# First attention scores placed between the value projection's last products, and the attention output's norm and transposes begun head by head in the last tiles

## The reference, cut to what matters

```python
# one layer; 512 latent tokens and 128 prompt tokens share the projections
proj = h @ w_in                                    # q_r k_r v_r g_r q_d k_d v_d gates
q_d = apply_rope(q_d, cos_d, sin_d); k_d = apply_rope(k_d, cos_d, sin_d)   # latent tokens only
# differential attention, 8 heads, two maps m of 64 columns each
s = einsum('bqhmd,bkhmd->bhmqk', q, k) * dh ** -0.5
p = softmax(s); a = p[:, :, 0] - lam * p[:, :, 1]
o = einsum('bhqk,bkhe->bqhe', a, v)
o_d = rmsnorm(o, diff_subln_g) * (1 - lam_init)    # per head, 128 columns
branch_d = o_d.reshape(B, L, 1024) @ w_diff_out
mix = (gate_r * branch_r + gate_d * branch_d) @ w_o
# then residual, RMSNorm, SwiGLU FFN, residual, final norm
```

## Time and profile before

| what | us |
|---|---|
| median of 3 runs (1314.15 to 1314.39) | 1314.18 |
| the profiled execution, its own time | 1314.83 |
| its span in the trace | 1313.2 |
| PE busy | 1263.9 (96%) |
| DVE busy | 798.2 (61%) |
| ACT busy | 487.5 (37%) |
| POOL busy | 307.6 (23%) |

### The profile page before, as it was taken

The page is one execution under the profiler, slowest core; times in us unless marked ns, Lnnn a source line. Parts: engine busy times, 40 slices in busy tenths (PEclk is TensorE's granted clock), DMA queues, the critical chain, the costliest instruction groups (busy, mean ns, idle before and its releaser), DMA issues.

```text
span 1313.2 us, 19818 instructions
## 1 busy us (share of the span) xinstructions
PE 1263.9 (96%) x7734; PEld 1155.6 (88%) x7734; DVE 798.2 (61%) x1292; ACT 487.5 (37%) x812; POOL 307.6 (23%) x269
## 2 busy tenths in 40 slices
PE   4999999999999999999799899999999999999997
PEld 2698887799999999988688799889998999989986
DVE  4654121466657733463799754378984689547966
ACT  5452223344331112222777532245441244313434
POOL 1011000311000111120699700003520355005500
PEclk9999999999999999999899999999999999999999
DMA  9634222144444434362000034220233122322222
GB/s 307 206 97 136 64 74 71 41 148 141 127 131 130 142 104 127 106 192 97 33 1 1 10 121 153 88 64 27 71 119 106 33 81 89 120 64 64 89 89 80
DMA packets 87392, 129.56 MB, mean 99 GB/s; under 512 B 3529, under 2 KB 64450, under 8 KB 87186
## 3 DMA queue, kind: packets, MB, share of 16 engines
q1 hardware_dynamic: 76880, 95.17, 22.7%
q0 software_dynamic: 9104, 32.20, 8.0%
q10 hardware_dynamic: 1330, 1.10, 0.3%
HBM read 117.43 MB, written 4.73 MB: 93 GB/s over the span
## 4 chain that ended last, share of the span: by engine, by line
PE 85%; POOL 6%; DVE 4%; ACT 3%; issue 1%; DMA 1%; SPq 0%; ACTq 0%; DVEq 0%
PE psum L421 31%; PE psum L458 28%; PE psum L664 17%; POOL probs L961 4%; POOL probs L967 3%; PE psum L1024 1%; PE psum L407 1%; DMA ada_a<-in_w_ada 1%; PE psum L594 1%; PE psum L522 1%; DVE w_lo L390 1%; PE psum L1132 1%; PE psum L1130 1%; PE psum L1131 0%; ACT probs L1531 0%
## 5 line engine op out<-in xcount | busy, mean ns | idle before, releaser
L390 DVE TENSOR_TENSOR w_lo<-w_raw,w_hi 128x2048 fp32r<-128x2048 f32 x57 | 130.6, 2291 | 200.9 <-ACT w_hi L385 197.6
L385 ACT ACTIVATE w_hi<-w_raw 128x2048 fp32r<-128x2048 f32 x57 | 108.8, 1909 | 173.7 <-PE psum L458 107.5
L421 PE MATMUL psum<-h_hi,w_lo 128*128 128x320 f32 x672 | 154.7, 311 | 0.8 <-ACT y_nat L1474 0.8
L421 PE MATMUL psum<-h_hi,w_hi 128*128 128x320 f32 x672 | 153.1, 309 | 0.0
L421 PE MATMUL psum<-h_lo,w_hi 128*128 128x320 f32 x672 | 153.0, 309 | 0.0
L458 PE MATMUL psum<-w_hi,hid 128*128 128x512 f32 x440 | 135.5, 389 | 0.0
L421 PEld LDWEIGHTS psum<-h_hi,w_lo 128*128 128x128 f32 x672 | 111.8, 188 | 1.7 <-issue 1.7
L421 PEld LDWEIGHTS psum<-h_lo,w_hi 128*128 128x128 f32 x672 | 112.3, 188 | 0.0
L421 PEld LDWEIGHTS psum<-h_hi,w_hi 128*128 128x128 f32 x672 | 112.3, 188 | 0.0
L664 PE MATMUL psum<-h_hi,seven_lo 128*128 128x320 f32 x320 | 98.9, 309 | 1.1 <-DVE silu_g L2189 1.1
L664 PE MATMUL psum<-h_lo,seven_hi 128*128 128x320 f32 x320 | 98.9, 309 | 0.0
(11 more groups left out here) (302 smaller groups left out, 2771.7 us busy)
## 6 DMA issues: line engine op xcount, KB each, us to landing
w_raw<-in_w_in SPq DMA_DIRECT2D x32, 1024.0 KB, 5.5
ada_b<-in_w_ada POOLq DMA_DIRECT2D x32, 512.0 KB, 4.0
w_raw<-in_w_ffn_gate SPq DMA_DIRECT2D x11, 1024.0 KB, 5.4
w_raw<-in_w_ffn_up SPq DMA_DIRECT2D x11, 1024.0 KB, 5.4
ada_a<-in_w_ada SPq DMA_DIRECT2D x8, 1024.0 KB, 13.3
w_raw<-in_w_ffn_down SPq DMA_DIRECT2D x8, 1024.0 KB, 5.1
w_raw<-in_w_ret_out SPq DMA_DIRECT2D x4, 1024.0 KB, 5.2
swapped<-qk_d POOLq DMA_DIRECT2D x32, 128.0 KB, 2.6
```

The costliest lines, as they stand in the source:

```text
L385: act.activation(w_hi[s][:, :, :], w_raw[s][:, :, :], ACT.Copy).then_inc(w_hi_done, 1)
L390: dve.tensor_tensor(w_lo[s][:, :, :], w_raw[s][:, :, :], w_hi[s][:, :, :].bitcast(F32), ALU.subtract).then_inc(w_lo_done, 1)
L421: last = pe.matmul(bank(4 * par + 2 * j + h, HALF), w[:, k, cs], x[:, k, h * HALF:(h + 1) * HALF], start=(k == 0 and n == 0), stop=(k == K ...
```

## The change

The change does the following, on each engine:

- **PE.** The waits for `rope_done` and for the cached keys come ahead of v_d. In v_d's last group both modulation sums stand at the end of the first half, followed by the scores of tile 0. In the second half the token tiles go in the order 0, 2, 1, 3, 4, with a transpose of the gate columns after tile 0, the scores of tile 1 after tile 1, and the scores of tile 2 after tile 3. The loop then begins at slot 2. The transposes of the prompt's keys go to slot QT+1, the first block of the output's transposes to slot QT+2.
- **ACT.** It copies v_d's last five tiles between the exponentials of tiles 0 to 2. The high part of diff_out's first unit is made in 4 parts in slots 8 to 11. The roots for heads 0 to 6 come in slot QT, the copy of the prompt's keys in slot QT+1, the root of head 7 after the first block.
- **DVE.** The late modulation begins once its four sums are copied. The low part of diff_out's first unit is made in 8 parts in slots 14 to 21. The means and inverses of heads 0 to 6 come in slots QT and QT+1, heads 0 to 3 are scaled in slots QT+1 and QT+2, heads 4 to 7 between the low parts. Its wait for the stored prompt keys goes from the prompt groups to diff_out.
- **POOL** issues the gate vector's DMA ahead of the attention and the prompt keys' DMA after it, and scales no heads. **SP** issues the prompt values' DMA, and loads diff_out's first weights once the transposes of tiles 0 to 2 are done, because the weights of tiles 0 to 2 (`first_probs`) lie over the two raw weight buffers.

```diff
+LAST_TILES = (0, 2, 1, 3, 4)
+EARLY_HEADS = 7
+ACT_SPLIT_SLOTS, DVE_SPLIT_SLOTS = range(8, 12), range(14, 22)
-        k_out = at("k_out", H + 16, [P, D])
+        k_out = at("k_out", H + 25, [P, D])
+        first_probs = at("first_probs", W, [P, 3, 2, TOK])
+        def weights_of(n, m):
+            return (first_probs if n < 3 else probs)[:, n % 3, m, :]
+        def dve_split_part(dve, unit, s, part, parts):
+            ks = slice(part * KT // parts, (part + 1) * KT // parts)
+            if part == 0:
+                dve.wait_ge(w_hi_done, unit + 1)
+            done = dve.tensor_tensor(w_lo[s][:, ks, :], w_raw[s][:, ks, :], w_hi[s][:, ks, :].bitcast(F32), ALU.subtract)
+            if part == parts - 1:
+                done.then_inc(w_lo_done, 1)
...
 # pe_wide
-                        for t in range(TILES):
+                        for t in LAST_TILES if between and (i, par) == (1, 1) else range(TILES):
+                            if between and (i, par) == (1, 1):
+                                between(t)
+                    if between and i == 1:
+                        if par == 0:
+                            pe.wait_ge(freed[r], START[name][r] + TILES)
+                            pe.wait_ge(ada_step, 16 * (ADA_FIRST[name] + 3) + 32)
+                            for slot in range(2):
+                                last = sums_over_partitions(pe, slot, bank(1, 4, 4 * slot))
+                            last.then_inc(mm_done, 2)
+                            between(None)
+                        else:
+                            last.then_inc(mm_done, 2)
+                        continue
...
 # PE
             pe_dense(pe, "k_d", pe_T_unit, h_hi, h_lo)
-            pe_wide(pe, "v_d", h_hi, h_lo)
-            pe.wait_ge(freed["act"], START["diff_out"]["act"])
             pe.wait_ge(rope_done, 12 + AHEAD)
-            for h in range(DH):
-                last = pe.transpose(bank(6 + h // 4, P, (h % 4) * P), qk_d[:, DH + h, LAT:TOK], ident[:, :])
-            last.then_inc(k_ps, 1)
-            pe.wait_ge(ld_vc, 16)
             pe.wait_ge(kc_done, 1)
 # scores(n)
+                if n == 1:
+                    pe.wait_ge(freed["act"], START["v_d"]["act"] + TILES + 3)
+                if n == 2:
+                    pe.wait_ge(ada_copied, 4)
 # PE loop
-            pe.wait_ge(k_copied, 1)
-            for slot in range(-1, QT + 4):
+            def early_scores(t):
+                if t == 0:
+                    pe.wait_ge(gate_cols_set, 2)
+                    pe.wait_ge(at_max, 1)
+                    pe.transpose(psum[0:4 * KT, BANK:BANK + P], gate_cols[:, :, :, :].rearrange("p g c m -> p (g c m)"),
+                                 ident[:, :]).then_inc(gate_T_ps, 1)
+                if t == 3:
+                    pe.wait_ge(gate_T_set, 1)
+                if t in (None, 1, 3):
+                    scores((None, 1, 3).index(t))
+            pe_wide(pe, "v_d", h_hi, h_lo, between=early_scores)
+            for slot in range(2, QT + 4):
                 if 0 <= slot - 3 < QT:
                     weights_T(slot - 3)
+                if slot == QT + 1:
+                    prompt_keys_T()
                 if 0 <= slot - 4:
                     outputs(slot - 4)
+                if slot == QT + 2:
+                    pe.wait_ge(k_copied, 1)
+                    pe.wait_ge(at_e, 2 * QT)
+                    pe.wait_ge(norm["normo"]["scaled"], 1)
+                    tiles_T(pe, "od", o_nat, 0, 2)
                 if slot + 1 < QT:
                     scores(slot + 1)
             pe.wait_ge(at_oe, QT)
+            pe_T_and_dense(pe, "od", o_nat, "diff_out", od_hi, od_lo, by_block=norm["normo"]["scaled"], begun=1)
...
 # ACT
+            act_split(act, unit_of("v_d", 1, 1), 1)
+            act.wait_ge(mm_done, 2 * unit_of("v_d", 1, 0) + 2 + AHEAD)
+            for par in range(2):
+                copy_ada("v_d", 1, par, bank(1, 4, 4 * par)).then_inc(ada_copied, 1)
             set_table(ACT.Exp)
+            act.wait_ge(w_lo_done, unit_of("v_d", 1, 1) + 1)
+            exp(0)
...
+            v_d_tiles(1, (0, 2, 1))
+            exp(1)
+            v_d_tiles(1, (3,))
+            exp(2)
+            v_d_tiles(1, (4,))
+            for slot in range(3, QT + 3):
+                evacuate_T(slot - 3)
                 if slot < QT:
                     exp(slot)
+                if slot in ACT_SPLIT_SLOTS:
+                    act_split_part(act, unit_of("diff_out", 0, 0), 0, slot - ACT_SPLIT_SLOTS.start, len(ACT_SPLIT_SLOTS))
                 if slot == QT:
                     set_table(ACT.Sqrt)
+                    root("normo", EARLY_HEADS * TILES)
+                if slot == QT + 1:
+                    keys_out()
...
 # DVE, behind factor, evacuate_o and maximum of the slot
+                if slot in DVE_SPLIT_SLOTS:
+                    dve_split_part(dve, unit_of("diff_out", 0, 0), 0, slot - DVE_SPLIT_SLOTS.start, len(DVE_SPLIT_SLOTS))
+                if slot == QT:
+                    head_means(0, EARLY_HEADS)
+                if slot == QT + 1:
+                    head_inverses(0, EARLY_HEADS, 1)
+                if QT < slot < QT + 3:
+                    for h in (2 * (slot - QT - 1), 2 * (slot - QT) - 1):
+                        scale_head(dve, h).then_inc(norm["normo"]["scaled"], 1)
+            head_means(EARLY_HEADS, DH)
+            for k in range(KT):
+                split_T(dve, "od", od_hi, od_lo, subln_gain, k)
+                if k + 4 == EARLY_HEADS:
+                    head_inverses(EARLY_HEADS, DH, 2)
+                if k + 4 < DH:
+                    scale_head(dve, k + 4).then_inc(norm["normo"]["scaled"], 1)
```

More of the change, by code:

```diff
@@ L71 @@
 WIDE_BANKS = ((0, 1, 2, 6, 7), (3, 4, 5, 6, 7))
+LAST_TILES = (0, 2, 1, 3, 4)
+EARLY_HEADS = 7
 def wide_ready(name, i, t):
-    return (2 * WIDE.index(name) + i) * LAT_TILES + t + 1
+    place = LAST_TILES.index(t) if (name, i) == ("v_d", 1) else t
+    return (2 * WIDE.index(name) + i) * LAT_TILES + place + 1
 def lay_out_phases():
@@ L438, in wide, with pe_wide @@
             return w[:, 2 * k:2 * k + 2, :].rearrange("p a b -> p (a b)")
-        def pe_wide(pe, name, hi, lo, kt=KT, split=None):
+        def pe_wide(pe, name, hi, lo, kt=KT, split=None, between=None):
             r, half = READER[name][0], kt // 2
@@ L531, in block @@
                 if by_block is not None:
[L532 removed]
+                    pe.wait_ge(by_block, k + 1)
                 tiles_T(pe, which, src, k, 2 + 2 * (k % 3))
[L535 removed]
+            for k in range(begun, 3):
                 if which == "yg":
@@ L737, in norm2_low, with act_to_T @@
             dve.tensor_tensor(h2_lo[:, k, cs], hf2[:, k, cs], h2_hi[:, k, cs].bitcast(F32), ALU.subtract).then_inc(q["lo"], 1)
-        def act_to_T(act, which, hi, scale):
+        def act_to_T(act, which, hi, scale, blocks=range(KT)):
             q = n2t[which]
-            for k in range(KT):
+            for k in blocks:
                 act.wait_ge(q["ps"], k + 1)
@@ L841, in _ @@
             stream_wide("v_d", w_in, 5120)
+            sp.wait_ge(freed["act"], START["diff_out"]["act"])
+            sp.dma_start(o["new_diff_v"][0, 0].rearrange("p h e -> p (h e)"), v_d[:, LAT_TILES, :]).then_inc(vd_stored, 16)
+            sp.wait_ge(at_T, 3)
             stream("diff_out", columns(by_tile["w_diff_out"], 0))
@@ L1195, in weights_T @@
                     out = last_keys_T(n) if c == LAT_TILES else bank(6, P, c * P)
-                    last = pe.transpose(out, probs[:, n % 3, 0, c * P:(c + 1) * P], ident[:, :])
+                    last = pe.transpose(out, weights_of(n, 0)[:, c * P:(c + 1) * P], ident[:, :])
                 last.then_inc(at_T, 1)
             def outputs(n):
+                if n == 0:
+                    pe.wait_ge(freed["act"], START["diff_out"]["act"])
+                if n == GROUPS:
+                    pe.wait_ge(ld_vc, 16)
                 pe.wait_ge(at_aT, n + 1)
@@ L1434, in copy_N, with evacuate @@
             def copy_N(name, dst, func, after=0):
-                def evacuate(i):
+                def evacuate(i, tiles=range(TILES)):
                     if after:
                         act.wait_ge(rope_done, after + AHEAD)
-                    for t in range(TILES):
+                    for t in tiles:
                         wait_tile(act, name, i, t)
-                        if name in ADA_FIRST and t == LAT_TILES:
+                        if name in ADA_FIRST and t == LAT_TILES and i == 0:
                             copy_ada(name, i, 1, bank(ada_wide_bank(i, 1), 4)).then_inc(ada_copied, 1)
@@ L1513, in _ @@
             dense("k_d", copy_T("k_d", qk_d, DH, 1.0))
[L1514 to L1517, removed]
+            v_d_tiles = copy_N("v_d", v_d, ACT.Copy, after=12)
+            dense_wide("v_d", v_d_tiles, groups=1)
             def exp(n):
@@ L1849, in dense_wide @@
                             following()
```

(11 more changed lines are left out.)

89 lines of the change are left out of this document (43 added, 46 removed).

## The result

| kernel | median, us | range | runs |
|---|---|---|---|
| before | 1314.29 | 1313.43 to 1315.90 | 6 |
| after | 1319.83 | 1319.27 to 1320.71 | 6 |

The changed kernel is slower by 0.43%: the ratio is 1.0043, with a 95% interval of 1.0032 to 1.0054. The forecast was 1320.6, the difference +6.4 against a measured +5.5. The profiled execution took 1319.99 us, with a span of 1318.3; before, the span was 1313.2. So the trace has to account for 5.1 us. The times of the kernel before fall into two groups (of its 17 runs beside experiments 5 to 8, ten took 1313.3 to 1314.8 us at a mean granted clock of 0.995, seven 1315.3 to 1316.3 at 0.991 or 0.992), and the changed kernel is slower than both.

What follows compares the result with a forecast made beforehand. PE bounds the kernel almost throughout, POOL the attention, with slots nearly full on four engines. 9.2 + 2.5 - 9.0 + 6.9 + 0.2 - 3.4 = +6.4 on 1314.18 gives 1320.6 us; whole range 1313.5 to 1325.5.

Steps and rivals of the forecast that it cites:

- Steps 1 and 2: PE at v_d's front: waiting for the last key rotation costs 9.2 us, the lowered clock after that pause 2.5.
- Step 3: v_d's second half: scores placed between its tiles let POOL start its latent tiles earlier, -9.0 us (bounds -7 to -10.7).
- by tile 4: First latent tiles: next scores wait for one transposed tile only and PE avoids half clock, another 0.5 us gained.
- Step 4: Attention slots 14 to 21: DVE's eight low parts wait for POOL's add and delay its next tile, 0.87 each, +6.9 us.
- Rival A: Attention slots: the split parts don't meet POOL's add and cost 1.2 us, total 1314.9, no measurable change; chance 0.12.
- Step 5: Attention slots 8 to 11: ACT's four high parts, about 0.5 each against 0.53 of idle time, cost +0.2 us.
- Step 6: Tail after POOL's end: earlier transposes, DVE scaling heads between tiles and no POOL scaling save 3.4 us.
- Rival B: PE in front of v_d: the rotation wait is short, so the kernel gets faster, 1308.9 us; chance 0.05.
- Rival C: Attention: slots suffer beyond the parts, each of 12 losing another 0.3 to 0.5, about +5, 1325 us; chance 0.13.

Runs made afterwards that it cites:

- experiments 5 to 8: Late-wait kernel with scores behind v_d (1318.52), scaling behind last tile (1311.46), or low part in two pieces (1305.48); kernel before plus only the wait ahead of v_d (1325.58).
- experiment 2: Changed kernel with DVE's low part as one 128x2048 instruction in slot 14 instead of eight parts in slots 14 to 21: 1316.47 us.
- Experiment 3: Changed kernel with DVE's eight subtractions replaced by maximum reductions over the same 128x256 raw weights, leaving out that low part: 1315.35 us.
- experiment 7: Changed kernel with the rotation wait in front of tile 0's scores and DVE's low part in two 128x1024 pieces, slots 14 and 15: 1305.48 us.
- Experiment 6: Changed kernel with the late rotation wait, heads 0 to 3 scaled and block 0 transposed only after all tiles are evacuated: 1311.46 us.
- experiment 1: Changed kernel with PE's rotation wait moved from the front of v_d to the front of tile 0's scores: 1308.34 us.
- experiment 4: Changed kernel with both the rotation wait in front of tile 0's scores and DVE's low part in one piece: 1306.36 us.

## Why the prediction was right, by its steps

The steps as forecast and as the two traces and the runs have them:

| step | forecast | trace | by itself |
|---|---|---|---|
| 1. wait for the rotation | +9.2 | +8.8 | 1 and 2 together: 11.5 and 10.9 |
| 2. clock behind it | +2.5 | +2.2 | |
| 3. early scores | -9.0 | -7.8 | about 10 |
| 4. DVE's eight parts | +6.9 | +5.5 | 3.4 less in one piece |
| 5. ACT's four parts | +0.2 | +0.2 | not tried |
| 6. tail | -3.4 | -3.7 | 3.1 |
| sum | +6.4 | +5.2 | medians: +5.5 |

*Steps 1 and 2* held. v_d's first product moved by 572.28 - 563.45 = 8.83; The wait itself costs 0.4 more, about 9.3, because k_d's last product started 0.44 earlier than before (562.72 against 563.16). PE's pause of 9.10 is counted from that product's end. By the sums PE is 11.0 late, so the clock took 2.2. The forecast's 2.5 lay between two shorter half-speed stretches; here the pause was longest, yet only 4.4 us of work ran at half speed: the clock stood at 0.50 from 568.9 on, while PE was still idle. This size isn't fixed. Experiments 2 and 3 have the same code up to this place. There the half speed lasted 5.3 and 6.1 us, and PE came to the sums at 618.06 and 618.38, so the clock took 2.5 and 3.0.

*Step 3* was the right mechanism with its size 1.2 too large. The forecast let PE go from the sums to the end of v_d in 19.4 us (606.64 to 626.0); it took 637.97 - 617.64 = 20.3. The wait for tile 1's copy came out as forecast (0.69 idle), and the exponentials of tile 0 ended in v_d's cover. What was too small is each change of work on PE. The sums took 1.77 to the next start instead of 1.56. The first scores took 1.09 instead of 0.9, and the first product behind them 0.34 to its successor instead of 0.23. The other 0.3 is the gain "by tile 4": from tile 2 to the first steady tile POOL took 652.35 - 641.45 = 10.9, against 649.12 - 638.01 = 11.1 before, 0.2 less and not 0.5. The value lay inside the bounds of -7 and -10.7. (The forecast's own steps give 627.3 + 2.0 = 629.3; it wrote 629.5.)

*Step 4* was the costliest mis-sizing, 1.4, and it too is one of size. The rule in the forecast (the part is held until POOL's add ends, then runs, then the factor) is exactly what the rows show. But behind the add the part needed only 0.20 to the next start (684.34 - 684.14), not the 0.33 that a part alone was put at, as if the first 0.13 of its work had passed while it was held. (The first part lasted 0.81 and the later ones 1.08, where the forecast said 0.9: DVE no longer waits for scores then and comes to the add earlier. They end with it all the same.) Experiments 2 and 7 give the same offset. 128x2048 takes 682.80 - 680.73 = 2.07 behind the add instead of 2.21, 128x1024 takes 669.54 - 668.54 = 1.00. So the slot costs 0.73, the eight cost 5.9. (8 times the forecast's 0.87 is 7.0, not 6.9.) The fixed part of the price is the factor: its 0.56 to POOL's start (684.90 - 684.34) runs under POOL's add in a usual slot, and here it comes behind it. Whether a part placed behind the factor would cost less wasn't tried.

The eight intervals are followed by three of 3.05, 2.93 and 2.95 instead of 3.10, and 0.4 came back, which the forecast hadn't foreseen. Two of POOL's scalings there took 1.60 instead of 1.72. The rows say when this happens: in the slot at 710.96 DVE's factor is ready at 710.37 + 0.27 = 710.64, 0.35 ahead of the end of POOL's add; in a steady slot it is ready 0.04 to 0.08 ahead. In the traces of both kernels, every scaling of 1.60 or 1.61 has its factor ready at least 0.24 ahead, at the attention's ends too (before: 652.17 and 735.83), and every one of 1.72 at most 0.10. So a slot of POOL's work alone is 2.93, and the steady 3.10 still holds something of the factor's late arrival. Why a factor that comes 0.07 ahead costs 0.17 isn't shown.

Rival A is ruled out by the changed kernel's own rows, since the parts do meet the add. Experiment 3 shows what eight instructions that don't wait for it cost, 0.7; the rival's 1.2 was put for a case that didn't occur.

*Step 5* is one interval of 671.03 - 667.75 = 3.28 in place of 3.10. It was read from the trace alone.

*Step 6* held within 0.3. Experiment 6 shows its main cause, the work moved between the last tiles (3.1 of 3.7).

*Rival B* asked for a short wait; the rotation ended where it had ended. Its time, 1308.9, is what experiment 1 reached by moving the wait (1308.34). *Rival C*, slots that suffer beyond the parts, is ruled out by the trace: from 652.35 on, apart from the eight slots and the one of step 5, POOL's intervals are 3.11 or shorter.

The forecast came out 0.8 high. Steps 3 and 4 were each too large in size (by 1.2 and 1.4) and of opposite sign, so their errors nearly cancel. The small error of the sum is partly such luck.

## What to carry to other kernels

Put a wait directly in front of its first user: at the head of an interleaved section everything behind it pays, here 9 us and then the clock, about twice what the rest of the change gained. Where GpSimd is busy through a whole slot, a two-operand VectorE instruction in front of the factor that GpSimd waits for paid a price here that doesn't depend on its size (0.54 us), so hand the work over in few large pieces, or find an instruction that doesn't wait for GpSimd, as the reduction did. But watch TensorE's clock with the largest piece: of two profiles with a pause of 1.9 us in the same slot, one kept the full clock and one lost about half of the saving.

## What the runs showed of the hardware that was not expected

- Cost of a piece of DVE work in a slot that POOL fills: 0.73 us for 128x256, 1.53 for 128x1024, 2.61 for 128x2048. All three fit one line: 0.54 plus the piece's time behind the add (0.20, 1.00, 2.07). The 0.54 is the factor's way to POOL (0.56), which a usual slot hides.
- A DVE reduction of 128x256 beside the same POOL add took 0.41 us, the subtraction of the same size 1.08.
- POOL's scaling of 128x512 took 1.60 us where DVE's factor was ready 0.23 us or more ahead of the end of POOL's add, and 1.72 where it was ready 0.11 ahead or less. This holds for every latent tile in the traces of both kernels and of all eight experiments.
- A pause of PE of 1.92 us (experiment 4) was followed by a granted clock of 0.65 over the next window. One of 1.93 in the same slot (experiment 2) was not, nor were those of 0.85 and 1.25 (experiment 7). The length of the pause alone doesn't decide.
- Behind the same pause of 9.1 us, at the same code, the half speed lasted 4.4, 5.3 and 6.1 us in three profiles (the changed kernel, experiments 2 and 3).
- Experiment 1, whose profile shows a granted clock of 1.00 from 560 to 752, spread over 0.6 us only. Which pause of the kernel before tips its clock isn't settled.
